# A decoder layer on one core: the gate product between two levels of q, and transposes in the middle of the next block's products

## The reference

```python
u = x * (1.0 + scale1) + shift1
p = u @ w_in                                   # 3*512 + 4*512 columns
y_conv = short_conv(cb, cc, cv)                # width 3, 512 channels
y_rec  = hgrn2(q, f, i, g)                     # 4 heads of 128, gated linear recurrence
#   o = o * rsqrt(mean(o^2) + eps) * gnorm_w * silu(g)
mix = concat(y_conv, y_rec) @ w_out
x = layer_norm(alpha * x + gate1 * mix)
u = x * (1.0 + scale2) + shift2
# top-1 of 4 groups, top-2 of its 8 experts; every expert:
#   h = silu(xblk @ w_gate[e]) * (xblk @ w_up[e]);  y = h @ w_down[e]
x = layer_norm(alpha * x + gate2 * moe(u))
```

## Time and profile before

| | |
|---|---|
| runs | 2064.24, 2065.76, 2067.18 us; median 2065.76 |
| profiled execution | 2080.12 us |
| its span, first to last instruction | 2078.2 us |
| mean granted clock of PE | 0.925 of full |
| PE, DVE, ACT, POOL busy | 1817.4, 1119.6, 612.9, 571.7 us |
| mixer, experts | about 90 to 1040 us, 1413 to 1953 us |
| blocks of experts | 50 (400 down matmuls, 8 each) |

### The profile page before, as it was taken

The page is one execution under the profiler, slowest core; times in us unless marked ns, Lnnn a source line. Parts: engine busy times, 40 slices in busy tenths (PEclk is TensorE's granted clock), DMA queues, the critical chain, the costliest instruction groups (busy, mean ns, idle before and its releaser), DMA issues. The chain is left out here.

```text
span 2078.2 us, 28737 instructions
## 1 busy us (share of the span) xinstructions
PE 1817.4 (87%) x9032; PEld 1401.5 (67%) x9033; DVE 1119.6 (54%) x1715; ACT 612.9 (29%) x746; POOL 571.7 (28%) x685
## 2 busy tenths in 40 slices
PE   6799999999999999999859999147999999999685
PEld 2487777777778889889748887115666666666431
DVE  3365555656565555565447775612456433355198
ACT  0432223222222222222121111102455443455233
POOL 0121112222222101222025444252334422334245
PEclk7899999999999999999979999567999999999897
DMA  9632322222322322232185452725899956689495
GB/s 337 201 87 81 86 83 82 87 86 74 89 80 79 90 73 77 84 89 71 38 260 176 148 160 94 240 55 158 288 323 368 371 174 226 204 281 334 157 394 197
DMA packets 295019, 341.88 MB, mean 165 GB/s; under 512 B 18631, under 2 KB 244424, under 8 KB 292476
## 3 DMA queue, kind: packets, MB, share of 16 engines
q1 hardware_dynamic: 271820, 283.37, 42.5%
q0 software_dynamic: 18000, 55.87, 7.4%
q10 hardware_dynamic: 5106, 1.42, 0.4%
HBM read 276.08 MB, written 64.55 MB: 164 GB/s over the span
## 5 line engine op out<-in xcount | busy, mean ns | idle before, releaser
L1401 DVE TENSOR_TENSOR w_gu_lo<-w_gu_raw,w_gu_hi (+1 forms) x64 | 146.3, 2290 | 142.5 <-ACT w_gu_hi L1394 141.5
L626 POOL TENSOR_TENSOR o_r<-o_ms,neg_half 128x4 f32<-128x4 f32 (+1 forms) x16 | 16.8, 1050 | 720.5 <-DVEq L862 720.5
L826 DVE TENSOR_TENSOR w_lo<-w_raw,w_hi 128x1024 fp32r<-128x1024 f32 x112 | 140.9, 1258 | 108.6 <-ACT w_hi L524 104.4
L678 PE MATMUL pr<-ub_hi,w_hi 128*128 128x288 f32 (+1 forms) x672 | 193.0, 341 | 0.0
L678 PE MATMUL pr<-ua_hi,w_hi 128*128 128x512 f32 x448 | 188.3, 420 | 0.0
L678 PE MATMUL pr<-ub_hi,w_lo 128*128 128x288 f32 (+1 forms) x672 | 187.6, 333 | 0.0
L678 PE MATMUL pr<-ub_lo,w_hi 128*128 128x288 f32 (+1 forms) x672 | 187.3, 333 | 0.0
L1909 PE MATMUL ph<-w_gu_hi,x_hi 128*128 (+1 forms) x408 | 177.2, 434 | 10.8 <-DVE x_lo L1866 10.4
L1932 PE MATMUL py<-w_dn_w,hhT 128*128 x400 | 184.8, 605 | 0.7
L678 PE MATMUL pr<-ua_lo,w_hi 128*128 128x512 f32 x448 | 182.2, 407 | 0.0
L678 PE MATMUL pr<-ua_hi,w_lo 128*128 128x512 f32 x448 | 182.0, 406 | 0.0
(11 more groups left out here) (338 smaller groups left out, 3417.0 us busy)
## 6 DMA issues: line engine op xcount, KB each, us to landing
w_raw<-in_w_in SPq DMA_DIRECT2D x112, 512.0 KB, 4.1
w_gu_raw<-in_w_e_gate SPq DMA_DIRECT2D x32, 1024.0 KB
w_gu_raw<-in_w_e_up SPq DMA_DIRECT2D x32, 1024.0 KB
w_dn_w<-in_w_e_down SPq DMA_DIRECT2D x32, 1024.0 KB
w_ring<-in_w_mod SPq DMA_DIRECT2D x10, 2048.0 KB, 19.3
y_t<-y_scratch SPq DMA_DIRECT2D x16, 1024.0 KB, 7.5
x_cols<-in_x_prompt SPq DMA_DIRECT2D x32, 256.0 KB, 4.9
y_raw<-y_scratch SPq DMA_DIRECT2D x16, 512.0 KB, 4.8
```

The lines of the kernel that those rows point to most:

```text
L626: pool.tensor_tensor(o_r[:, 0:c], o_ms[:, 0:c], keep["neg_half"][:, 0:c], ALU.pow).then_inc(o_rs, 1)
L678: last = pe.matmul(pr[n % 2][:, a * 512:a * 512 + c], w[:, n % WS, k, :], x[:, k, a * c:(a + 1) * c], start=(k == 0 and m == 0), stop=(k = ...
L826: dve.tensor_tensor(w_lo[:, n % WS], w_raw[:, n % WRAW], w_hi[:, n % WS].bitcast(F32), ALU.subtract).then_inc(lo_done, 1)
L1401: dve.tensor_tensor(w_slot(keep["gu_lo"], s, lo, hi), w_slot(keep["gu_raw"], r, lo, hi), w_slot(keep["gu_hi"], s, lo, hi).bitcast(F32), AL ...
```

## The change

In the mixer, `recurrent_out(u - 1)` is called after the second level of q (l = 1) and not after the split of job n+4. In the experts, `x_hi` and `x_lo` get two slots, chosen by the block's parity; steps 2 and 3 of PE's list move into the middle of `gate_up(g+1)`, ahead of its fifth slice and of its wait for the second half of the weights; ACT makes `x_hi` of block g+2 before the sigmoid of block g+1, and DVE makes `x_lo` of g+2 before the gate product of g+1. Ahead of the loop, the transposes of block 1 move into the middle of `gate_up(0)`.

```diff
@@ -979,6 +979,8 @@
                         dve.tensor_tensor(dst[:, :, 1, :], src[:, :, 1, :], wleft, ALU.mult)
                         dve.tensor_copy(dst[:, :, 0, :], src[:, :, 0, :])
                         dve.drain().then_inc(q_lev, 1)
+                        if l == 1 and u:
+                            recurrent_out(u - 1)
                     if u == FIRST_S:
                         dve.wait_ge(proj_done, NT * FIRST_S)
                         dve.memset(qs_msk[:, :], 0.0)
@@ -990,8 +992,6 @@
                     if u < FIRST_S:
                         low_u(q)
                     split_lo(n + 4)
-                    if u:
-                        recurrent_out(u - 1)
                     if u < FIRST_S:
                         low_u(q + 1)
                     split_lo(n + 5)
@@ -1703,8 +1703,8 @@
         ps = lambda name, shape: ctx.enter_context(nc.psum_tensor(name, shape, F32))
         sem = lambda name: ctx.enter_context(nc.semaphore(name))
         xg = sb("xg", [P, 2, D])
-        x_hi = sb("x_hi", [P, KT, P], F32R)
-        x_lo = sb("x_lo", [P, KT, P], F32R)
+        x_hi = sb("x_hi", [P, 2, KT * P], F32R)
+        x_lo = sb("x_lo", [P, 2, KT * P], F32R)
         gsig = sb("gsig", [P, DE])
         gsil = sb("gsil", [P, DE])
         hh = sb("hh", [P, DE])
@@ -1830,9 +1830,9 @@
                         act.wait_ge(gu, last + 1)
                     split_high(act, keep, e, a, act.snap(e % 2), act.snap(e % RAW))
 
-                def x_evac(b):
+                def x_evac(b, half):
                     act.wait_ge(xT_ps, b + 1)
-                    act.activation(x_hi[:, :, :], px[:, :].rearrange("p (k t) -> p k t", k=KT), ACT.Copy).then_inc(x_h, 1)
+                    act.activation(x_hi[:, bass.ds(half, 1), :].rearrange("p a w -> p (a w)"), px[:, :], ACT.Copy).then_inc(x_h, 1)
 
                 def sigmoid(b):
                     act.wait_ge(gu, b + 1)
@@ -1841,8 +1841,8 @@
                 def block_work(g, gu_next):
                     act.wait_ge(hT, g + 1)
                     act.activation(hhT[:, :, :], pht[:, 0:KD * P].rearrange("p (k t) -> p k t", k=KD), ACT.Copy).then_inc(hT_sb, 1)
+                    x_evac(g + 2, act.snap(g % 2))
                     sigmoid(g + 1)
-                    x_evac(g + 2)
                     if gu_next is not None:
                         split_gu(gu_next, 1)
                     act.wait_ge(dn, g + 2)
@@ -1850,9 +1850,9 @@
                     act.activation(y_sb[:, :], py[:, :], ACT.Copy, scale=ids_cur[:, 2:3].bitcast(F32)).then_inc(y_rdy, 1)
 
                 act.sem_inc(y_rdy, 1)
-                x_evac(0)
+                x_evac(0, 0)
+                x_evac(1, 1)
                 sigmoid(0)
-                x_evac(1)
                 expert_loop(act, split_gu, block_work)
 
             @block.vector
@@ -1861,9 +1861,10 @@
 
                     split_low(dve, keep, e, a, dve.snap(e % 2), dve.snap(e % RAW))
 
-                def x_evac(b):
+                def x_evac(b, half):
                     dve.wait_ge(x_h, b + 1)
-                    dve.tensor_tensor(x_lo[:, :, :], px[:, :].rearrange("p (k t) -> p k t", k=KT), x_hi[:, :, :].bitcast(F32), ALU.subtract).then_inc(x_l, 1)
+                    dve.tensor_tensor(x_lo[:, bass.ds(half, 1), :].rearrange("p a w -> p (a w)"), px[:, :],
+                                      x_hi[:, bass.ds(half, 1), :].rearrange("p a w -> p (a w)").bitcast(F32), ALU.subtract).then_inc(x_l, 1)
 
                 def gate(b):
                     dve.wait_ge(sig, b + 1)
@@ -1872,14 +1873,14 @@
                     dve.tensor_tensor(hh[:, :], ph[:, DE:GU], gsil[:, :], ALU.mult).then_inc(h_rdy, 1)
 
                 def block_work(g, gu_next):
+                    x_evac(g + 2, dve.snap(g % 2))
                     gate(g + 1)
-                    x_evac(g + 2)
                     if gu_next is not None:
                         split_gu(gu_next, 1)
 
-                x_evac(0)
+                x_evac(0, 0)
+                x_evac(1, 1)
                 gate(0)
-                x_evac(1)
                 expert_loop(dve, split_gu, block_work)
 
             @block.tensor
@@ -1897,32 +1898,38 @@
                         last = pe.transpose(px[:, k * P:(k + 1) * P], xg[:, half, k * P:(k + 1) * P], ident[:, :])
                     last.then_inc(xT_ps, 1)
 
-                def gate_up(b, e, s):
+                def gate_up(b, e, s, half, mid):
                     pe.wait_ge(gu_l, 2 * e + 1)
                     pe.wait_ge(x_l, b + 1)
                     if not (isinstance(b, int) and b == 0):
                         pe.wait_ge(h_rdy, b)
                     for k in range(KT):
                         if k == KT // 2:
+                            mid()
                             pe.wait_ge(gu_l, 2 * e + 2)
                         for m, (x, w) in enumerate(((x_hi, gu_hi), (x_hi, gu_lo), (x_lo, gu_hi))):
-                            last = pe.matmul(ph[:, :], x[:, k, :], w_slot(w, s, k * GU, (k + 1) * GU),
+                            last = pe.matmul(ph[:, :], x[:, half, k * P:(k + 1) * P], w_slot(w, s, k * GU, (k + 1) * GU),
                                              start=(k == 0 and m == 0), stop=(k == KT - 1 and m == 2))
                     last.then_inc(gu, 1)
 
                 pe.sem_inc(dn, 1)
                 transposes(0, 0)
-                gate_up(0, 0, 0)
-                transposes(1, 1)
-                def block_step(g, half):
-                    e_now, e_next = expert_of(g), expert_of(g + 1)
-                    s_down, s_next = pe.snap(e_now % RAW), pe.snap(e_next % 2)
-                    gate_up(g + 1, e_next, s_next)
+                gate_up(0, 0, 0, 0, lambda: transposes(1, 1))
+
+                def hidden_transposes(g):
                     pe.wait_ge(h_rdy, g + 1)
                     for k in range(KD):
                         last = pe.transpose(pht[:, k * P:(k + 1) * P], hh[:, k * P:(k + 1) * P], ident[:, :])
                     last.then_inc(hT, 1)
-                    transposes(g + 2, half)
+
+                def block_step(g, half):
+                    e_now, e_next = expert_of(g), expert_of(g + 1)
+                    s_down, s_next = pe.snap(e_now % RAW), pe.snap(e_next % 2)
+
+                    def between():
+                        hidden_transposes(g)
+                        transposes(g + 2, half)
+                    gate_up(g + 1, e_next, s_next, 1 - half, between)
                     pe.wait_ge(hT_sb, g + 1)
                     pe.wait_ge(wd_in, 16 * e_now + 16)
                     pe.wait_ge(y_rdy, g + 1)
```

## The result

Four runs of the changed kernel took 1977.51 to 1982.93 us, **median 1979.48**; the kernel before, run beside it, 2065.28. The ratio is **0.9585, 95% interval 0.9569 to 0.9602**: 86 us less. The forecast was 1978, with a range of 1964 to 1998. The profiled execution took 1982.93 us, with a span of 1980.2.

A forecast was written before the change was run, and what follows sets the result against it. The prediction took TensorE (PE), busy 87% of the span, as the bound, with gains where it stands still or runs at its lower clock. Mixer 83 and experts 5 make 88 us: 2065.8 - 88 = 1977.8, so 1978 us, range 1964 to 1998.

The forecast's parts named there:

- The waits of the mixer: Mixer, line 703: PE's 15 waits of the v transposes for `y_rec` go entirely, 55 us.
- The clock: Mixer: PE's half-speed stretches behind 13 of the 15 waits go, 13 x 2.2 = 29 us.
- The bounds of 27 to 36: Mixer: second count of the clock loss, from the mean clock of 0.96 over 884 us, less some 4 inside waits.
- What is late next: Mixer: later splits leave 1.6 us of cover at the scores; up to 1 us back in the sample-converting unit.
- The second wait in the mixer: Rival: cover used up, PE waits at line 695 for `pa`; 16 to 24 us back, 1994 to 2002; chance 0.11.
- The mixer's sum: Mixer: 55 of waits + 29 of clock - 1 given back = 83 us.
- The wait for `hhT`: Experts: 0.11 us before the down product goes in 38 of the 50 blocks, 4 us; bounds 0 and 8.
- The first blocks: Experts: two `x_lo` waits of 2.5 us each; gain 1 us, between 0 and 2.5.
- The ring: Experts, one-block stretches: a cycle closing without PE stays at 11.0 us a block; gain 0 us.
- The prediction's 5 us for this: Experts: without the DVE/POOL lock, `ids_cur` would end some 0.4 us sooner in 12 blocks, 5 us.
- The carried difference: Whole kernel: median of runs shown, 2065.8, lies 14.3 us below the profiled 2080.1; carried over to the forecast.
- The sum: Whole kernel: mixer 83 + experts 5 = 88 us; 2065.8 - 88 = 1977.8; forecast chance 0.76.

The follow-up runs named there:

- m_l4: Kernel before with the mixer's edit alone, but the gate product placed after the fifth level of q (l = 4): 1998.32 us, ratio 0.9660 to the kernel before.
- m_l6: Kernel before with the mixer's edit alone, but the gate product placed after the seventh level of q (l = 6): 2030.14 us, ratio 0.9825 to the kernel before.
- x_only: Kernel before with the experts' edit alone, the mixer unchanged: 2059.02 us, ratio 0.9955 to the kernel before.
- m_only: Kernel before with the mixer's edit alone, the experts unchanged: 1988.67 us, ratio 0.9606 to the kernel before.
- after_again: The changed kernel run once more, as base for follow-up kernels beside it: 1977.61 us, ratio 0.9569 to the kernel before.
- hid_mid: Changed kernel with only the `hh` transposes in the middle; x transposes behind the products, ACT and DVE in old order: 1978.77 us, ratio 0.9570 to the kernel before.
- cur2: Changed kernel with two slots for `ids_cur` alone; `y_sb` still waits for the scatter's landing: 1970.68 us, ratio 0.9536 to the kernel before.

## Why the prediction was right, step by step

**The waits of the mixer** were sized at 55 us by the step from issue to issue; 54.9 by the same count over all 15 units, and none is left. The reason was the one given: m_l4 to m_l6 bring the wait back at about 0.75 us a level of q.

**The clock** was sized at 29 us. In the profiled execution it was 28.4, in 13 of the 15 waits, both as counted in the prediction. m_l6 shows that "half speed behind such a wait" is a frequency and not a rule, so another execution gives another sum: x_only, with the same waits, lost 22.4. By medians, 80.9 us in m_only less 54.9 of waits leaves 26, give or take 4. The bounds of 27 to 36 were drawn from one execution and do not hold for another, as the 22.4 shows.

**What is late next** in the mixer was given as up to 1 us in the unit that converts the samples. It was 0.3 us at line 695, there. The cover in unit 5 was 2.0 us where 1.6 was worked out. The second wait in the mixer, the strongest rival, did not come.

**The mixer's sum**: 83 predicted, 81.8 in the trace, 80.9 us by medians in m_only.

**The wait for `hhT`** was mis-sized: 0.11 us a block from the gap in front of the down product, 0.19 measured (10.22 to 10.03). The step that failed is "the missing 0.11 is the wait for `hhT`": only the start of the down product was read, not its first step, which holds another 0.09. The sum had 4 us where 0.19 x 35 = 7 was on offer, since 35 blocks ran at 10.2 before. Part of it was given back: 17 blocks took about 11 us in the changed kernel and 14 before, one of them (block 37, 11.48 us) behind a single late landing; it took 12.0 us in x_only and `after_again`, but not before and not in hid_mid. Predicted for the experts: 5; measured: 6.3.

**The first blocks** were to give 1 us, "there `x_lo` is early now". They gave 0.8, but the reading was half wrong: the first wait for `x_lo` stayed at 2.5 us, and only the second became a wait for the gate product, 1.7 instead of 2.5.

**The ring** was sized at 0 and came out at 0: 11.02 before, 11.01 to 11.03 after in all but two blocks (11.30 and 11.28), with the name in the list changed as forecast. The rule of the Trainium skill ("SBUF — State Buffer", the section on the two separate sides) that a DVE instruction with two SBUF inputs and a GpSimd one that reads SBUF exclude each other for the whole instruction is borne out by this case beyond the 0.04 us of the earlier trace rows. POOL's copy of 2 KB takes 0.20 us alone and 1.66, 1.72 and 1.97 beside a split, ending 0.04 to 0.05 us behind it each time (1469.84 + 1.97 = 1471.81, the split 1469.48 + 2.29 = 1471.77). In the changed kernel's trace all 27 of these copies that last over 0.4 us end 0.03 to 0.05 us behind a split. cur2 gives the price of the copy in this ring, its own 0.20 us included: 8.7 us. The prediction's 5 us for this was 0.4 us a turn, read from the end of the copy; with the copy out of the way a turn gives 1.0 us, until the weights are late.

**The carried difference.** 14.3 us between the profiled execution and the median of before were carried over. That was right for the median: 10.4 us of the profiled execution lay in routing, and no other trace has them. It also means that the forecast for the profiled execution, 1992.1, was 9.2 too high.

**The sum**: 88 predicted, 85.8 and 91.2 measured in two sets of runs.

## What to carry to other kernels

A wait of PE on a small operation of another in-order engine is priced at its idle time plus the half-speed stretch that follows it, and here the second was half as large as the first; when one moves the operation, a few places ahead are enough and each place has a price that can be measured. A stop in front of a group of matmuls should be read up to the group's second step, not its first. Where a ring of several engines sets a period, swapping two of its members changes only the name in the wait list; look for the member that stands in it for a side reason (here a 2 KB copy that needs a slot) and give that one a second slot.

## What was not expected of the hardware

- Whether the clock falls behind a wait of PE follows no fixed rule in these traces, but goes with the wait's length: 0 of 34 waits up to 1.9 us, 10 of 19 from 2.1 to 3.2, 21 of 22 from 3.7 to 4.6. Each fall cost 1.3 to 3.0 us. With the same waits, two executions differed by 6 us.
- A stop of 0.12 us in front of a matmul cost another 0.09 us inside the group behind it.
- With the ring open, 20 us of the one-block stretch hold 20.00 us of PE work with DMA at 378 GB/s and a share of 1.06, as in the closed ring (377 and 1.06): DMA that looks full did not hold a faster pace back for seven blocks; in the eighth ACT stood 3.06 us for weights.
